# A hybrid layer step on one core: state space parts reordered, tables issued by ScalarE, one-hots of a dense tile split between two engines

## What is computed

```python
h = x + W_out[concat(shortconv(xn), ssd(xn))]      # xn = RMSNorm(x); ssd: 8 heads of 64, state 128
h = h + CrossAttn(RMSNorm(h), memory K/V)          # 4 heads, 256 memory tokens
h = h + PEER(RMSNorm(h))                           # 8 heads, top 16 of 128 x 128 experts
y = RMSNorm(h)

# ssd, per token and causal:
y_diag = einsum('bclsg,bclsgh,bcsghp->bclghp', CB, Lm, xdt)   # Lm = exp(segment sums), masked
hT = decay * h + B^T xdt                                      # carried over the chunks
# peer, per token: eidx, gate from two top-16 lists of 128 keys
hid = gelu(einsum('td,thkd->thk', x, u_tab[eidx]))
out = einsum('thk,thkd->td', gate * hid, v_tab[eidx])
```

## Time and profile before

| | us |
|---|---|
| median of 3 runs (lowest, highest) | 1853.81 (1848.23, 1864.87) |
| the profiled execution | 1853.36 |
| its span in the trace | 1851.3 |
| TensorE busy | 1690.1 |
| VectorE busy | 1224.9 |
| GpSimd busy | 693.5 |
| ScalarE busy | 372.9 |

### The profile page before, as it was taken

One profiled execution on the slowest core, in us unless ns is written; L12 is line 12 of the kernel. 1 busy time (PEld: TensorE's weight loads), 2 busy tenths in 40 slices (PEclk: granted clock), 3 DMA queues, 4 the chain that ended last, 5 costly groups with the idle time before them and its releaser, 6 DMA issues. The chain is left out here.

```text
span 1851.3 us, 19837 instructions
## 1 busy us (share of the span) xinstructions
PE 1690.1 (91%) x7088; PEld 1256.2 (68%) x7088; DVE 1224.9 (66%) x2437; ACT 372.9 (20%) x914; POOL 693.5 (37%) x598
## 2 busy tenths in 40 slices
PE   6998999989747998899887999999999999999996
PEld 5887888877635676687776566666666666666542
DVE  1262211699687868798986899776656666656675
ACT  2032123111321244551661001101000000000101
POOL 0000000134123438640755455555444544444551
PEclk9999999999877998899989899999999999999998
DMA  5532443679244968994999999999999999999995
GB/s 167 173 114 91 159 137 127 232 244 363 81 154 154 363 222 303 353 364 138 331 356 414 410 408 410 409 408 409 410 410 410 402 409 410 397 410 403 381 402 228
DMA packets 238300, 563.09 MB, mean 304 GB/s; under 512 B 17068, under 2 KB 125276, under 8 KB 236156
## 3 DMA queue, kind: packets, MB, share of 16 engines
q0 software_dynamic: 82944, 302.03, 42.3%
q1 hardware_dynamic: 122236, 243.04, 35.9%
q10 hardware_dynamic: 33024, 16.78, 3.0%
HBM read 539.46 MB, written 21.66 MB: 303 GB/s over the span
## 5 line engine op out<-in xcount | busy, mean ns | idle before, releaser
L770 POOL DMA_INDIRECT M<-in_u_tab,IDX x288 | 324.8, 1128 | 743.5 <-DVE PEER L1717 361.0
L777 POOL DMA_INDIRECT M<-in_v_tab,IDX x288 | 365.1, 1268 | 383.2 <-DVE X L1738 308.3
L1079 PE MATMUL PSB<-XN,M 128*128 128x256 f32 x2048 | 468.6, 384 | 9.8 <-ACT M L1289 4.5
L1087 PE MATMUL PSB<-M,HST 128*128 128x512 f32 x1024 | 460.8, 596 | 12.0 <-DVE HST L1800 10.7
L1079 PEld LDWEIGHTS PSB<-XN,M 128*128 128x128 f32 x2048 | 393.5, 193 | 109.9 <-issue 52.6
L1717 DVE CUSTOM_DVE_ANT_0 M<-M,XN 128x1024 f32<-128x1024 f32 x288 | 351.5, 1222 | 144.4 <-DMA M<-in_u_tab,IDX 125.1
L1738 DVE SCALAR_TENSOR_TENSOR X<-M,PEER,X 128x1024 f32<-128x1024 f32 x256 | 327.8, 1281 | 107.3 <-DMA M<-in_v_tab,IDX 94.0
L819 PE MATMUL PSB<-M 128*128 128x256 f32 (+1 forms) x1408 | 334.1, 399 | 10.7 <-DVE M L1376 9.4
L1087 PEld LDWEIGHTS PSB<-M,HST 128*128 128x128 f32 x1024 | 195.0, 191 | 216.2 <-issue 200.4
L819 PEld LDWEIGHTS PSB<-M 128*128 128x128 f32 x1408 | 271.4, 194 | 67.1 <-DVE M L1376 10.3
L826 PE MATMUL PSB<-M 128*128 128x256 f32 (+1 forms) x1056 | 250.3, 398 | 6.0 <-DVE X L1591 5.4
(11 more groups left out here) (213 smaller groups left out, 1038.4 us busy)
## 6 DMA issues: line engine op xcount, KB each, us to landing
M<-in_u_blocks SPq DMA_DIRECT2D x128, 512.0 KB
M<-in_v_tab SPq DMA_DIRECT2D x128, 512.0 KB
M<-in_w_in SPq DMA_DIRECT2D x24, 1024.0 KB
M<-in_w_pq SPq DMA_DIRECT2D x16, 1024.0 KB
gate_spill<-M ACTq DMA_DIRECT2D x16, 1024.0 KB
M<-gate_spill SPq DMA_DIRECT2D x16, 1024.0 KB
M<-in_w_out SPq DMA_DIRECT2D x8, 1024.0 KB
M<-in_w_mq SPq DMA_DIRECT2D x8, 1024.0 KB
```

Of the source, the lines that this page charges most:

```text
L770: pool.indirect_dma_start(out=UA[:, s % RR, :], out_offset=None, in_=utab, in_offset=bass.IndirectOffsetOnAxis(ap=IDX[:, n:n + 1], axis=0) ...
L777: pool.indirect_dma_start(out=VA[:, s % RR, :], out_offset=None, in_=vtab, in_offset=bass.IndirectOffsetOnAxis(ap=IDX[:, n:n + 1], axis=0) ...
L1079: last = pe.matmul(PSB[:, 4 + b % 2, 0:2 * P], UBLK[:, b % SR, c, :], XN[:, 1:3, c * P:(c + 1) * P], start=(c == 0), stop=(c == DC - 1))
L1087: last = pe.matmul(PSB[:, 2 * t + hf, :], WR[:, b % WRING, t * P:(t + 1) * P], VBLK[:, b % SR, hf * 512:(hf + 1) * 512], start=(b == 0), s ...
```

## The change

1. State space part: s1 and s2 of the next tile come ahead of s4 of this one (before, s1 alone did), s2b is an entry of the order, and the products between are dealt out anew.
2. Start: ScalarE issues the nine small tables and the state; it does one Sqrt on a scratch column before its first entry. The state's transposes and drains are an entry of their own behind the first four `gc` products.
3. The one-hot buffers go round by one count over both tiles: two until the attention scores of tile 4, then three in tile 1, four in tile 2.
4. In tile 1 VectorE compares key 2 only (128x512), and ScalarE makes the gated one-hot alone: |iota - key 1| into the buffer (Abs), then Relu(gate - gate * that), with -gate in BACK. The planner counts 0.7 us for such an `oh`, 1.25 before. TensorE waits for both engines. The second `tt` waits until all batches of tile 1 are made.

The diff goes through the planner first, then SyncE's and ScalarE's start, TensorE's `gb`, ScalarE's `oh`, VectorE's `tt` and `oh`. SyncE's lines for the nine tables and the state are deleted where they stood.

```diff
-    order = [("s1", tiles[0])]
+    order = [("s1", tiles[0]), ("s2", tiles[0])]
     for t, after in zip(tiles, tiles[1:] + [None]):
-        order += [("s2", t), ("s3", t)] + ([("s1", after)] if after else []) + [("s4", t)]
+        order += [("s2b", t), ("s3", t)] + ([("s1", after), ("s2", after)] if after else []) + [("s4", t)]
...
-        if part in ("s2", "s3"):
-            s += [(part + "b", t)]
+        if part == "s3":
+            s += [("s3b", t)]
...
+            s += [("state",)] * (b == "gc") + [("memn", "gc v".split().index(b))]
...
-        s += soft_chain(TG[0], {("s1", 0): kv[0:1], ("s2", 0): kv[1:2], ("s1", 1): kv[2:4], ("s4", 0): kv[4:5], ("s2", 1): kv[5:7],
+        s += soft_chain(TG[0], {("s1", 0): kv[0:1], ("s2", 0): kv[1:3], ("s2", 1): kv[3:5], ("s4", 0): kv[5:7],
                                 ("s3", 1): kv[7:9], ("s4", 1): kv[9:10]})
...
-        s += soft_chain(TG[1], {("s1", 2): z[0:1], ("s2", 2): z[1:2], ("s1", 3): z[2:3], ("s2", 3): o[2][0:1], ("s1", 4): o[2][1:2],
-                                ("s2", 4): o[2][2:3], ("s3", 4): o[3][0:2], ("s4", 4): o[3][2:3]})
+        s += soft_chain(TG[1], {("s1", 2): z[0:1], ("s2", 2): z[1:2], ("s2", 3): z[2:3], ("s4", 2): o[2][0:1], ("s2", 4): o[2][1:3],
+                                ("s4", 3): o[3][0:1], ("s3", 4): o[3][1:3]})
...
 def dve_us(x):
+    if x[:2] == ("oh", DENSE[0]):
+        return 0.7
...
+def hot_places():
+    at, last, turn = {}, {}, 0
+    for seg in PLAN:
+        if seg == ("a1", NP):
+            free = PLAN.index(seg)
+    for n, seg in enumerate(PLAN):
+        if seg[0] == "oh":
+            k = (2 if n < free else 3 if seg[1] == DENSE[0] else 4)
+            at[seg[1:]] = (turn % k, last.get(turn % k))
+            last[turn % k] = ("gb",) + seg[1:]
+            turn += 1
+    return at
...
+                act.dma_start(SMR[r:r + src.shape[0], :], src).then_inc(small_in, 16)
+            act.dma_start(S0[:, :, :], a["state_ssd"].rearrange("l b (x h) p n -> (h p) (l b x) n", h=2)).then_inc(state_in, 16)
             act.wait_ge(const_ok, 1)
+            act.activation(PSM[:, 0:1], EPSC[:, :], ACT.Sqrt)
...
                 pe.wait_ge(oh_done, m + 1)
+                pe.wait_ge(hot_done, m + 1)
...
             def oh(t, n):
...
+                if d == 0:
+                    if n == 0:
+                        wait_drained(act, ("tt", 1))
+                    before = HOT[t, n][1]
+                    if before in SMALL:
+                        act.wait_ge(oh_used, SMALL.index(before) + 1)
+                    elif before:
+                        wait_job(act, before)
+                    elif HOT[t, n][0] == 2:
+                        wait_job(act, ("s", NP, 1))
+                    for j in range(OH_TOK):
+                        away = act.activation(hot[:, j, 0, :], iota[:, :], ACT.Abs, bias=TT[:, 0, 0, c + j:c + j + 1], scale=-1.0)
+                    link(away)
+                    for j in range(OH_TOK):
+                        last = act.activation(hot[:, j, 0, :], hot[:, j, 0, :], ACT.Relu, bias=TT[:, 0, 2, c + j:c + j + 1],
+                                              scale=BACK[:, c + j:c + j + 1])
...
             def tt(t):
...
+                    link(dve.tensor_scalar(BACK, b[:, 2 * P:3 * P], -1.0, None, ALU.mult))
                 else:
                     dve.wait_ge(tt_done, 1)
+                    dve.wait_ge(oh_done, P // OH_TOK)
...
+                if d == 0:
+                    part = [P, OH_TOK, P]
+                    dve.tensor_tensor(hot[:, :, 1, :], bc(iota[:, :].unsqueeze(1), part), bc(TT[:, 0, 1, c:c + OH_TOK].unsqueeze(2), part),
+                                      ALU.is_equal).then_inc(hot_done, 1)
+                    return
```

More of the change, by code:

```diff
@@ L290, in jobs_of @@
     if k == "const":
-        return [("sm", "D"), ("hi", "D")]
+        return [("sm", "D")]
+    if k == "state":
+        return [("hi", "D")]
     if k == "turn":
@@ L837, in const, with state @@
                 transposes("sm", [SMR[:, :]])
+            def state():
                 pe.wait_ge(state_in, 16)
@@ L1293, in oh @@
                 m, c = d * P // OH_TOK + n, n * OH_TOK
-                act.wait_ge(hot_done, m + 1)
-                for j in range(OH_TOK):
-                    first = hot_buffer(t, n)[:, j, 0, :]
-                    last = act.activation(first, first, ACT.Copy, scale=TT[:, d, 2, c + j:c + j + 1])
+                hot = hot_buffer(t, n)
+                if d == 0:
[14 more added lines that the diff above has]
+                                              scale=BACK[:, c + j:c + j + 1])
+                else:
+                    act.wait_ge(hot_done, m + 1)
+                    for j in range(OH_TOK):
+                        last = act.activation(hot[:, j, 0, :], hot[:, j, 0, :], ACT.Copy, scale=TT[:, 1, 2, c + j:c + j + 1])
                 last.then_inc(oh_done, 1)
@@ L1814, in final @@
                 dve.scalar_tensor_tensor(out=x, in0=x, scalar=rs, in1=GAIN[0:n, :], op0=ALU.mult, op1=ALU.mult).then_inc(y_norm, 1)
-            does = {"const": const, "norm": norm, "turn": turn, "memn": memn, "in": in_, "keep": keep, "ca": ca, "cs": cs, "dt": dt, "oc": oc,
+            does = {"const": const, "state": state, "norm": norm, "turn": turn, "memn": memn, "in": in_, "keep": keep, "ca": ca, "cs": cs, "dt": dt, "oc": oc,
                     "kt": kt, "s1": s1, "s2": s2, "s3": s3, "s4": s4, "o": residual("o"), "a1": a1, "mo": residual("mo"),
```

38 lines of the change are left out of this document (15 added, 23 removed).

## The result

The changed kernel takes 1866.26 us (median of 11 runs, 1857.21 to 1869.45) against 1853.43 us for the kernel before on the same chip (11 runs): a ratio of 1.0058, with a 95% interval of 1.004 to 1.0077 (this and the ratios below are not plain quotients of the medians, which would be 1.0069 here). So it is a little slower, within 1%. The forecast was 1,858 us in a range of 1,838 to 1,877. The profiled execution's span went from 1851.3 to 1866.4 us, 15.1 us more, and that is the sum taken apart here.

What follows compares the result with a forecast made beforehand. The prediction took TensorE, busy for 91% of the span, as the bound, with slack only ahead of the last stage. Its terms, -1.8 + 0.6 - 9 + 15 = +4.8 us, gave 1,858 us, range 1,838 to 1,877.

Steps and rivals of the forecast that it cites:

- The bound: Last stage: TensorE is always busy, work unchanged, so a microsecond won or lost before about 870 us is one at the end.
- Start: Kernel start: tables land at 8.5 us, tile 0 starts earlier, memory norm loses 0.8 us; -1.8 us (0 to -3).
- Group 0: State space part, group 0: one TensorE wait goes, a new 1.6 us wait for DA comes; +0.6 us (-1 to +2).
- Group 1: State space part, group 1: VectorE's stalls for the exponential and the Relus shrink; -9 us (-2 to -18).
- The bound of -18: Group 1's best case: the granted clock, 0.82, rises with the filled gaps and TensorE's part of the loss goes too.
- One-hots: Tile 1, projection and pq: ScalarE's serial loop of 8.0 us per pair, 2.93 us a batch, makes TensorE wait; +15 us.
- Rival (a): One-hots: ScalarE's loop is cheap, pairs fall more under other products, 0 to +4 us; 1,845 us in all, chance 26%.
- Rival (b): One-hots: gaps lower the granted clock in the projection and Relu takes 2.0; +24 us, 1,877 us in all, chance 12%.
- Rival (c): State space reorder only moves the wait to the rows of s4; -2 us for -9, 1,865 us in all, chance 10%.
- (d): Both work: start -3, group 0 0, group 1 -16, one-hots 0 us; 1,834 us in all, chance 12%.
- the bounds of the one-hots (0 to +23): Tile 1's one-hots: +23 us with Relu at 2.0, 0 if VectorE's relief also clears the holes behind late gathers.
- the likeliest case: The forecast's own case for the whole kernel, 1,858 us: alone 1,851 to 1,866 us, chance 40%.

Runs made afterwards that it cites:

- One kernel with the old start: Kernel before with only the planner's price for an oh of tile 1 raised from 1.25 to 1.6 us: 1844.73 us, ratio 0.9952.
- The comparison kernel: Changed kernel with VectorE comparing both keys of tile 1 again and ScalarE scaling, at the old price of 1.25 us: 1839.71 us, ratio 0.9931.
- the order alone: Kernel before with only the new order of the state space parts, without the entry for the state: 1842.02 us, ratio 0.993.
- part 4 alone: Kernel before with only ScalarE making tile 1's gated one-hots, planner's price 0.7, two buffers, old order and start: 1871.14 us, ratio 1.0101.
- The table of runs: Changed kernel at prices 0.7, 1.25, 1.6: comparison as before, ratios 0.9987, 0.9931, 0.9862; ScalarE alone, 1.0058, 0.9958, 0.9948.
- the fastest kernel: The comparison kernel with the planner's price for an oh of tile 1 at 1.6 us instead of 1.25: 1829.08 us, ratio 0.9862.

## Why the prediction held, point by point

**The bound** held: the last stage kept its length (984.2 and 985.4 us), so what was lost ahead of `lk` 0 was lost at the end in the profiled executions.

**Start, -1.8, measured -4.2.** The landing of the tables was put at 8.5 us; it was 9.57. The sentence on the Trainium skill's DMA: Bandwidth & Descriptors, section "Issuing engines are not separate DMA queues", had it right: the same landing from either queue (9.57 and 9.48 us). From the landing on, the path was right: the prediction allows 1.9 us to the first token transposes (its terms, 0.42, 0.3 and 0.95, add up to 1.67) and they took 1.77, so the lead of 1.65 us is its own bound for a landing at 9.5. The state's transposes ahead of the memory norm cost 0.2 us and not 0.8. That makes 1.5 us. The other 2.7 had no term: TensorE's matmuls up to s1 of the first tile took 2.3 us less (the first 64 products alone 15.66 us for 16.92). One kernel with the old start shows such a saving too, so errors of opposite sign met here, and the largest may be chance.

**Group 0, +0.6, measured +0.2.** As reckoned, with the new wait of 1.86 us for DA (1.6 expected).

**Group 1, -9, measured -4.8** in the profiled run and about -5.7 over all profiles. The mechanism was right: no wait is left at the exponential's successor (L1596), and the stalls for the Relus were 7.53, 2.64 and 2.97 us (2.9 each expected for the last two). The step that failed is the turn from VectorE's saving into the length of the stretch. TensorE's idle time fell by 11.4 us, even more than 9, but its matmuls took 6.7 us longer, 4.2 of these at L945 and L951, behind the new waits, where the granted clock is down to 0.50 (504 to 512 us). The bound of -18 named the clock as a gain only; it acted as a loss.

**One-hots, +15, measured +21.5.** The durations held: Relu 482 ns (0.47 to 0.48 expected), a batch 2.87 us (2.93), loops 7.3 to 8.9 us from 723 us on (8.0; the three before took 9 to 12), TensorE's wait for them 24.5 us (27), clock 0.90 in the projection. So 12.6 of the 15 us are there. The step that failed is what was left out: 5 us of waits elsewhere (5.6 us for the norm's rows where it was 3.1, and 3.2 us at L986 where it was 0.5), and 3.8 us of slower matmuls. The waits elsewhere don't come from ScalarE's lateness. The comparison kernel, whose one-hots are hardly late, has them too (L825 and L984 there):

```profile
PE PSB L825 <- DVE XN L1435: 5.2, 1, 5.2
PE PSB L984 <- ACT M L1239: 3.4, 1, 3.4
```

So has the order alone (6.6 and 3.0 us), while part 4 alone in the old order has 4.4 and 0.5. They mostly came with the new order, to which the prediction gave nothing in this stage.

**The cause inside that term** is where the reasoning was most off. The prediction counted the planner's 0.7 in half a sentence, as what puts a pair in front of nearly every product, and gave the whole loss to ScalarE's 2.93 us. The table of runs shows ScalarE's work alone to be worth 5.3 us of stage; the price alone costs 13.2; 8 us come only where the two meet. The 8 us are the weakest of these: at 1.6 ScalarE's work costs 10.1 us, and a stage's matmuls alone differ by several us between kernels. Rival (a), the cheap loop, would have been right at a price of 1.25: that kernel ran at 1843.29 us, against the rival's 1,845. Rival (b) had the clock lost in the gaps: the 3.8 us are that, far from its +11.

**Rivals (c) and (d)** fell: the new order is worth 0.7% by itself. Rival (c)'s 1,865 us lie closer to the 1866.26 than the forecast's 1,858, but by chance: it had the order fail and the one-hots at +15. Only part of the order's 0.7% is the state space part; 4 to 5 us lie in the one-hots' stage (250.0 us before, 246.0 with the order alone), where the order moved the plan from 22 to 24 products. The prediction had no term for that.

**The total.** On the spans +4.8 us were forecast and +15.1 came, 10.3 more: -2.4 from the start, -0.4 from group 0, +4.2 from group 1, +6.5 from the one-hots and +2.4 from the two places that had no term. It lay inside the range since the bounds of the one-hots (0 to +23) and of group 1 (-18 to -2) held what they had to hold. At the edge of the likeliest case (1,851 to 1,866) it owes something to luck: the start gave 2.4 us more than forecast, and the extra waits of the one-hots' stage were covered by a bound that was made for the length of a Relu.

## What to carry to other kernels

Where a planner weaves by estimated costs, an estimate is a spacing: here lowering one packed the work more closely, whatever the instructions cost. Before moving work between engines, count how many host products the woven work falls under before and after, and set against it everything that is woven in with it (here the gathers). One number in the table, 1.25 to 1.6, gave 0.5% in the kernel before. With the new order and the new start it took the kernel from 0.7% to 1.4% ahead of the kernel before, on four executions; with ScalarE's one-hots it gave nothing. The third buffer and the issue queue gave nothing, and ScalarE's one-hots lengthened the stage at each of the three prices. Look past the stage, too: in the fastest kernel the wider spacing left VectorE late at the start of the next stage.

## What the runs showed of the hardware

The activation with one pointer operand (Abs with a bias, 128x128) takes 389 ns and the one with two (Relu with bias and scale) 482 ns: 93 ns for the second, after 79 for the first. By ScalarE: Activation LUTs of the Trainium skill, section "What ACT_TABLE_LOAD costs", a pointer operand is about 93 ns; the trace agrees for the second, and has 79 for the first. Rows, changed kernel, 680 to 880 us:

```profile
L1327 ACT ACTIVATE PEER<-PEER 128x128 f32<-128x128 f32 x80 | 33.0, 482 | 0.7
L1324 ACT ACTIVATE PEER<-iota,PEER 128x128 f32<-128x128 f32 x80 | 25.4, 389 | 2.2 <-ACT M L1353 2.2
...
L1298 ACT ACT_TABLE_LOAD x2 | 2.6, 1283 | 0.0
```

The two table loads there are those of the gelu, as before; Abs and Relu brought none. Not expected was how far one stretch of unchanged instructions moves between kernels: 92.2 to 97.9 us of TensorE work in group 1 over the ten profiles with the new order, with the granted clock at 0.85 to 0.80. The longest of the ten was 4.6 us off their mean, so a difference of that size between two single profiles of such a stage is not yet a finding.
